# Eight adaptive vectors: from thin TensorE products to row sums on VectorE

## The reference, cut to what matters

```python
def ada_params(cond, w_ada, b_ada):
    return jnp.split(jax.nn.silu(cond) @ w_ada + b_ada, 6, axis=-1)
...
        sh1_l, sc1_l, g1_l, sh2_l, sc2_l, g2_l = [m[:, None, :] for m in ada_params(c, w_ada[l], b_ada[l])]
        h_l = rmsnorm(x_l, norm1_g[l]) * (1.0 + sc1_l) + sh1_l
        y_l, y_c = token_mixer(h_l, h_c, ...)
        x_l = x_l + g1_l * y_l
        h2_l = rmsnorm(x_l, norm2_g[l]) * (1.0 + sc2_l) + sh2_l
        x_l = x_l + g2_l * routed_moe(h2_l, ...)
```

## Time and profile before

| | us |
|---|---|
| median of 3 runs | 862.99 (861.13 to 866.02) |
| the profiled execution | 862.04 |
| its span, first to last instruction | 860.3 |
| TensorE busy | 775.3 (90%) |
| VectorE busy | 523.3 (61%) |
| ScalarE busy | 423.0 (49%) |
| GpSimd busy | 197.5 (23%) |
| mean granted TensorE clock | 0.973 |

### The profile page before, as it was taken

One profiled execution on the slowest core, in us unless ns is written; L12 is line 12 of the kernel. 1 busy time (PEld: TensorE's weight loads), 2 busy tenths in 40 slices (PEclk: granted clock), 3 DMA queues, 4 the chain that ended last, 5 costly groups with the idle time before them and its releaser, 6 DMA issues.

```text
span 860.3 us, 15936 instructions
## 1 busy us (share of the span) xinstructions
PE 775.3 (90%) x6396; PEld 634.1 (74%) x6396; DVE 523.3 (61%) x780; ACT 423.0 (49%) x749; POOL 197.5 (23%) x362
## 2 busy tenths in 40 slices
PE   3998997999979999799779898998999999999975
PEld 1678886799858997599768778887777777687631
DVE  1488585457843578445564446668977675786143
ACT  3476653448425484245822445465666565673101
POOL 3003261103801137022230103011241223212201
PEclk9999998999989999899988999999999999999998
DMA  9969469535695366844867558863889999999992
GB/s 312 290 204 270 118 163 209 152 87 138 171 202 135 86 170 151 217 124 128 273 134 184 175 148 261 346 259 113 299 347 420 408 420 420 417 418 366 419 418 118
DMA packets 182021, 208.37 MB, mean 242 GB/s; under 512 B 50212, under 2 KB 155341, under 8 KB 169017
## 3 DMA queue, kind: packets, MB, share of 16 engines
q1 hardware_dynamic: 179833, 203.28, 72.8%
q0 software_dynamic: 2112, 4.04, 1.2%
HBM read 190.64 MB, written 20.22 MB: 245 GB/s over the span
## 4 chain that ended last, share of the span: by engine, by line
PE 59%; DMA 12%; DVE 10%; POOL 7%; issue 5%; ACT 4%; SPq 2%; POOLq 0%; ACTq 0%; DVEq 0%
PE bank L2512 57%; DMA raw<-in_w_e_dram 5%; POOL lane L980 3%; POOL lane L978 2%; SPq L619 2%; DVE w_lo L2197 2%; DMA half_raw<-in_w_in_dram 2%; PE bank L2515 2%; DMA lane<-problem_rows 2%; DMA problem_rows<-lane 1%; DMA raw<-in_w_ada_dram 1%; DVE chan L1833 1%; DVE half_lo L1737 1%; ACT lane L1292 1%; DMA mix_raw<-in_a_w_s_dram 1%
## 5 line engine op out<-in xcount | busy, mean ns | idle before, releaser
L2512 PE MATMUL bank<-hT,half_hi 128*128 128x256 f32 (+1 forms) x1024 | 226.6, 316 | 8.5 <-issue 4.8
L2512 PEld LDWEIGHTS bank<-hT,half_hi 128*128 128x128 f32 x1024 | 164.7, 189 | 24.5 <-issue 8.7
L2512 PE MATMUL bank<-hT,half_lo 128*128 128x256 f32 (+1 forms) x512 | 158.3, 309 | 0.0
L1737 DVE TENSOR_TENSOR half_lo<-half_raw,half_hi 128x1024 fp32r<-128x1024 f32 x88 | 108.3, 1231 | 50.3 <-ACT half_hi L1169 49.4
L2197 DVE TENSOR_TENSOR w_lo<-raw,w_hi 128x2048 fp32r<-128x2048 f32 x36 | 88.2, 2458 | 46.8 <-ACT w_hi L1602 46.8
L1169 ACT CAST half_hi<-half_raw 128x1024 fp32r<-128x1024 f32 x88 | 91.9, 1048 | 41.2 <-PE bank L2512 22.4
L2512 PEld LDWEIGHTS bank<-lane 64*64 64x64 f32 (+3 forms) x1968 | 82.0, 149 | 33.5 <-issue 19.6
L2512 PE MATMUL bank<-lane 64*64 64x64 f32 (+3 forms) x1968 | 90.3, 239 | 16.6 <-issue 12.7
L2512 PEld LDWEIGHTS bank<-hT,half_lo 128*128 128x128 f32 x512 | 97.1, 190 | 7.2 <-issue 1.9
L1602 ACT CAST w_hi<-raw 128x2048 fp32r<-128x2048 f32 x36 | 68.7, 1909 | 34.6 <-PE bank L2512 19.9
L1833 DVE SCALAR_TENSOR_TENSOR chan<-bank,conv_col,chan 128x508 f32<-128x508 f32 (+3 forms) x96 | 63.2, 658 | 10.3 <-ACT chan L1240 7.7
(11 more groups left out here) (386 smaller groups left out, 1352.6 us busy)
## 6 DMA issues: line engine op xcount, KB each, us to landing
raw<-in_w_e_dram SPq DMA_DIRECT2D x96, 1024.0 KB, 10.8
half_raw<-in_w_in_dram SPq DMA_DIRECT2D x64, 512.0 KB, 5.0
half_raw<-in_w_ada_dram SPq DMA_DIRECT2D x32, 512.0 KB, 4.7
raw<-in_w_ada_dram SPq DMA_DIRECT2D x8, 1024.0 KB, 11.5
dense<-staged SPq DMA_DIRECT2D x32, 128.0 KB, 4.6
half_raw<-in_w_proj_a_dram SPq DMA_DIRECT2D x8, 512.0 KB, 5.9
half_raw<-in_w_proj_b_dram SPq DMA_DIRECT2D x8, 512.0 KB, 5.0
half_raw<-in_w_out_dram SPq DMA_DIRECT2D x8, 512.0 KB, 6.3
```

The source lines that it names most:

```text
L1737: dve.tensor_tensor(half_lo[m % HBUF][:, :], half_raw[n % HRING][:, :], half_hi[m % HBUF][:, :].bitcast(F32), ALU.subtract).then_inc(s["ha ...
L2512: return nc.tensor.matmul(dst, lhsT, rhs, start=start, stop=stop)
```

## The change: who sums the weight rows, and where

For the eight late vectors the thin products are gone. VectorE multiplies each row block by its column of the conditioning and adds it to a 128x512 sum `ada_sum`, two operations for each half (`ada_steps`), eight a vector; each waits for the one before. The first takes as addend `ada_first`, which is zero but for row 0, into which SP loads the bias of that vector (`load_ada_bias`). One product with a column of ones adds the 128 partitions (`ada_fold`), into bank 0 or 3, and ScalarE copies that row (`ada_line_copy`), where it copied twice. `ada_taken` is now counted by VectorE. On SP `ada_halves` of the first vector come after `move_inverse`, all four, where two stood before it.

```diff
+            def load_ada_bias(m):
+                if m:
+                    sp.wait_ge(s["ada_taken"], 4 * m - 3)
+                load(ada_first[0:1, :], b_ada[0, 2 * D + m * N:2 * D + m * N + N].unsqueeze(0), s["landed_bias"])
...
                 move_solved()
-                ada_halves(2 * i + 0, 0, 2)
                 move_inverse()
-                ada_halves(2 * i + 0, 2, 4)
+                ada_halves(2 * i + 0, 0, 4)
+                load_ada_bias(2 * i + 1)
                 after_split(CHAN_AT[j, 4])
...
-                act.copy(ada_sums, bank[3][0:97, :]).then_inc(s["ada_copied"], 1)
...
+            def ada_steps(m, first, last):
+                for c in range(first, last):
+                    n = ADA_AT[m] + c
+                    dve.wait_ge(half_landed[n % HRING], 16 * (n // HRING + 1))
+                    if c == 0:
+                        dve.wait_ge(s["landed_bias"], 16 * m + 16)
+                        if m:
+                            dve.wait_ge(s["ada_folded"], m)
+                    else:
+                        dve.wait_ge(s["ada_taken"], 4 * m + c)
+                    rows_of = two(half_raw[n % HRING])
+                    own.after(dve.scalar_tensor_tensor(out=ada_sum[:, :], in0=rows_of[:, 0, :], scalar=cols[:, 2 * c:2 * c + 1],
+                                                       in1=(ada_sum if c else ada_first)[:, :], op0=ALU.mult, op1=ALU.add))
+                    dve.scalar_tensor_tensor(out=ada_sum[:, :], in0=rows_of[:, 1, :], scalar=cols[:, 2 * c + 1:2 * c + 2],
+                                             in1=ada_sum[:, :], op0=ALU.mult, op1=ALU.add).then_inc(s["ada_taken"], 1)
...
                 taps(4)
+                ada_steps(2 * i + 0, 0, 2)
+                silu(4)
+                ada_steps(2 * i + 0, 2, 4)
                 ahead(CHAN_AT[j, 4])
-                silu(4)
                 masks()
...
                 last_copy()
+                ada_steps(2 * i + 1, 0, 4)
                 ahead(DENSE_AT[3 + 7 * i + 3])
                 new_state(0)
...
             def ada_fold(m):
-                pe.wait_ge(s["ada_copied"], m + 1)
...
+                pe.wait_ge(s["ada_taken"], 4 * m + 4)
+                mm(ada_bank(m)[0:1, :], ones[:, 0:1], ada_sum[:, :]).then_inc(s["ada_folded"], 1)
```

97 lines of the change are left out of this document (38 added, 59 removed).

## The result

The changed kernel is slower: 874.31 us median of 19 runs (866.92 to 880.3) against 863.09 (858.16 to 868.65, 19 runs) before, ratio 1.0124 with a 95% interval of 1.0104 to 1.0144 (the run of 880.3, over 1.5% above the fastest, is a slow one and stays out of the ratio). I had forecast 867.5. The sign was right and the size was not: +11.2 us where I had +4.5. The profiled execution took 871.42 us (span 869.7) against 862.04 (860.3), so the traces show 9.4 of the 11.2.

What follows compares the result with a forecast made beforehand. POOL, SP and the DMAs bringing the inverse bound the kernel ahead of level_p, VectorE next at the updates. Terms +2.1, +0.3 and +2.3 gave +4.7 on the profiled 862.04, stated as 867.5 us median, range 855 to 877.

Steps and rivals of the forecast that it cites:

- The inverse and the masks: Loop iterations: level_p about 3 us earlier, but later H1's split holds masks and updates; +0.7 us each, three times, +2.1.
- Rival 2: At level_p and level_up: H1 lands early enough that the earlier inverse counts; -3.0 us three times, 856.3 us; chance 0.20.
- my bounds of 143.1 and 145: First iteration: H1 landing before about 143.1 gains time; masks starting before 145 would prove the forecast wrong.
- Vector 2i+1: Behind last_copy: sums fit VectorE's gap, but H3's refill, landing and split take 8.9 us ahead of new_state(0); +0.3 in all.
- Pair 3: Last pair: sums between recurrence links delay new_state(1) by 1.7 us and new_state(2) by 2.9 in all; +2.3 after savings.
- my sign that the +2.3 goes: Beside the last pair: if VectorE never waits for B1 to land, that loss of 2.3 us does not occur.
- The duration: VectorE's 64 chained operations over 512 columns: 0.72 us each, bounds 0.62 and 1.02, 46 us for all eight vectors.
- The rest: ScalarE loses one copy a vector, SP gets eight bias loads, POOL's memset moves to the start; 0 us.
- Rival 1: At level_up and behind: an emptied TensorE falls to half speed, level_up 7.4 us; +10.8, 873.8 us; chance 0.17.
- my section on the clock: Around level_p and level_up: TensorE stops twice, but by the rows nothing more falls to half speed; sum unchanged.

Runs made afterwards that it cites:

- e5: e1 with VectorE's masks, taps(5), silu(5) ahead of the split of H1, updates ahead of H2's, and ScalarE's tanh(5) ahead of both roundings: 857.99 us, ratio 0.9956.
- e1: Changed kernel, but in each loop iteration ScalarE rounds half H3 behind dense_copy and new_value(0), not ahead of them: 865.25 us, ratio 1.0019.
- e7: Changed kernel, but in the last pair VectorE's B sums stand behind the new states, branches and residuals: 864.3 us, ratio 1.0034.
- e6: Changed kernel, but in the last pair TensorE folds vector 6 ahead of branch_a(5) and state_sum(1): 872.38 us, ratio 1.0133.
- e14: e6 with the bias row of vector 7 issued behind two of the pair's four refills: 869.81 us, ratio 1.0089.
- e4: Changed kernel with all sums but a vector's first cut to 16 of 512 columns, for timing alone: 869.75 us, ratio 1.0074.
- e15: Changed kernel with an unused tile of 32 bytes a partition behind fold, weight buffers at 21792 as before: 883.12 us, ratio 1.025.
- e17: Changed kernel with an unused tile of 64 bytes a partition behind fold, weight buffers at 21824: 881.87 us, ratio 1.0219.
- e16: Kernel before the change with an unused tile of 32 bytes a partition behind fold_bias, weight buffers at 21824: 858.7 us, ratio 0.9948.
- e10: The edits of e5 and e7 together in one kernel, on the changed kernel: 850.78 us, ratio 0.9868.
- e13: Changed kernel with 7, 3, 8 and 8 unread products added in TensorE's waits ahead of turn_channels(3), level_p, level_up and z_part(0, 0): 872.38 us, ratio 1.0109.
- e2: Changed kernel with VectorE's masks ahead of the split of H1, not behind it: 874.16 us, ratio 1.0108.
- e3: Changed kernel, but in the last pair VectorE does the new states ahead of the B sums, residuals still behind them: 871.24 us, ratio 1.0122.

## Why the prediction was wrong in size

*The inverse and the masks (+0.7 three times).* Right as a mechanism: `level_p` at 138.66, near 140; the masks behind a split of H1 that begins at 143.93, near 145; `level_up` within 0.1 us of its old distance; the updates a wait ahead of `quarter_p`. Rival 2 fell: H1 landed at 142.85 and the masks began at 145.07; with the head start of 1.69 us these are 144.5 and 146.8 in before's times, later than my bounds of 143.1 and 145. The size came out otherwise. Up to the start of `last_up` (from `key_state(1)` of the iteration before, in the first one from the end of `channels(3)`) after takes 1.9 us less, 1.0 more and 1.1 less than before, together -2.0 where I had +2.1. What I had not seen is a stand of TensorE in before, in the midst of the dense product ahead of `last_up`, of 1.83, 1.68 and 1.28 us (the 4.8 of "issue" in before's page). It is gone in after, and the profile names nothing that it waited for; without it the sum would be +2.8. e5 says that the two splits hold back 1.8 us per iteration. With the 0.7 I had measured against before, not against what the earlier inverse could have given, so the two numbers don't exclude each other.

*Vector 2i+1 (+0.3 in all).* This is the step that failed. I wrote that H3's refill, landing and split come to 8.9 us, ahead of `new_state(0)`, and priced VectorE alone. H3 also passes ScalarE, whose rounding comes first and stands ahead of the `staged` copy and `new_value(0)`; behind those stand `z_part` and `state_sum(0)`. My own row had it: the split at 161.96 waited for ScalarE's `half_hi`. From the start of `last_up` to `key_state(1)`, in us:

| iteration | before | after | e1 |
|---|---|---|---|
| 1 | 7.24 | 11.07 | 8.37 |
| 2 | 8.53 | 12.29 | 8.39 |
| 3 | 7.26 | 11.18 | 8.36 |

So this stretch costs 11.5 us in the profiled executions, where I had 0.3 in all. The waits for `staged` are 2.42, 2.08 and 2.54 us, 7.0 together. The fold of vector 2i+1 is the second part, 1.0 us each: I had counted it as gone from ahead of `last_p`, and it has only moved here (167.04 in iteration 1). e1 takes 9.4 us of it back: the 7.0 of waits, about 1.6 of half clock behind the wait of iteration 2, and smaller gaps. By the medians e1 gets back 1.05%, about 9 us.

*Pair 3 (+2.3).* The places were right (both new states behind B sums), the reason of the first was not: 5.9 us in the traces, of which e7's trace has 4.8 back. VectorE never waits for B1, my sign that the +2.3 goes; the loss came all the same, by another way. I had +1.7 at `new_state(1)` from B1's landing; it was +4.1 (4.41 against 0.27), because B0's sum waits for the fold and then for the bias row (e6, e14), which I had priced at nothing. That both vectors share one accumulator, handed over by a fold that stands behind `branch_a(5)` and `state_sum(1)`, is not in my working at all. At `new_state(2)`, from B3's landing, I had +1.2 more, and it was +1.7.

*The duration (0.72 us).* 0.75, pitch 0.8: near, and by e4 a narrower sum would win back 0.5% at most by the medians, with both intervals overlapping.

*The rest (0).* In the profiled pair 6.0 us came back outside of all terms (-1.7, -1.6 and -2.7 in the table of landmarks). That the total stayed at +11.2 is partly luck: at before's addresses (e15) the change costs 2.5%, some 20 us, four times my sum, and with both kernels at 21824 (e17 against e16) 2.7 points, some 23 us.

*Rival 1, the half clock.* The clock does fall more often (5.2 us more lost in the iterations), which my section on the clock had ruled out: `level_up` takes 5.50 us, not 7.4 and not 4.61. As the cause of the whole loss the rival is out, since e1 wins 9 us by the medians with only 1.6 us less at half speed (13.3 against 14.9 in these stretches), and e10 is 1.3% faster than before though it loses 13.2 us to the half clock there, before 9.7. What the falls cost by themselves is open: e13 moved the fall from `level_up` to `last_p` and did not remove it, and its interval leaves room for a gain of 0.6%. The rows show both cases: the fall at `level_up` stands ahead of a wait and costs nothing (e13), the one behind the wait at `z_part` of iteration 2 costs about 1.6 us (12.29 less its wait of 2.08, against 11.18 less 2.54 in iteration 3, where the clock stays up).

The Trainium skill, "TensorE: Matmul & The Clock Gate", section "HAM oscillation — how this bites in real kernels", describes a fall of the clock at each wait for a DMA. Here the waits are for VectorE and ScalarE, and the trace agrees only in part: behind the wait of 3.76 us the granted clock is 0.50, as below, but behind that of 2.42 us in iteration 1 the products run at full speed, and behind that of 2.08 us in iteration 2 they do not.

```profile
147.00:148.00 1.00, 1.00 (x24) 0.50 0.91 348
```

(Stretch, its length in us, TensorE's busy share, granted clock, DMA share, GB/s.) Such a fall costs nothing where a wait for another engine stands behind it that ends at its own time.

## What to carry to other kernels

When a load becomes late, list every engine that touches it and what stands behind that touch in each in-order queue; the engine that only rounds or copies can cost more than the one whose work has grown. When a wait is taken away, move everything that stands behind the late thing (e5, e7), not the first item (e2, e3), or the wait appears one step further on. And before an edit of 1% is judged, shift the tiles by an unused one and time that too. A wait filled with idle products is no test of the clock until the next wait is looked at as well (e13).
